# Pairs of split activations moved by 2 to 7 lines of 64 bytes against the weights

## What is computed

```python
# first block: modulation, then three branches of one projection
hx, hc = modulate(rms_norm(x), sh1, sc1), modulate(rms_norm(ctx), csh1, csc1)
... = split_cols(hx @ w_in)             # attention, gated delta rule, gates
x = x + g1 * merge_branches(attn_x, gdn_x, gate_x, w_pa, w_pd, w_out)
x = x + g2 * conv_ffn(modulate(rms_norm(x), sh2, sc2), w_up, ffn_conv_w, ffn_conv_b, w_down)
# second block, two layers
u = rms_norm_2(h, norm1_g[l]); proj = u @ w_in[l]      # pool, differential attention, GLA
h = h + mix @ w_out[l]
z = rms_norm_2(h, norm2_g[l])
h = h + jnp.square(jax.nn.relu(z @ w_mlp1[l])) @ w_mlp2[l]
return rms_norm_2(h, final_norm_g)
```

## Time and profile before

| | |
|---|---|
| median of 3 runs | 2678.33 us (2673.72 to 2687.87) |
| profiled execution | 2682.11 us, its span 2680.3 us |
| mean granted TensorE clock | 0.975 |
| TensorE matmul busy | 2577.4 us, 96% of the span |
| weight loads busy | 2081.2 us, 78% |
| VectorE, ScalarE, GpSimd busy | 1399.7, 1023.4, 277.2 us |
| instructions | 46124, of them 19758 matmuls |

### The profile page before, as it was taken

How to read it: one execution, slowest core, us unless ns; L and a number is a source line. 1 busy time by engine, 2 the same in 40 slices (tenths; PEclk the granted TensorE clock), 3 DMA queues, 4 the chain that set the end, 5 groups by cost and what they waited for, 6 DMA issues and landing times.

```text
span 2680.3 us, 46124 instructions
## 1 busy us (share of the span) xinstructions
PE 2577.4 (96%) x19758; PEld 2081.2 (78%) x19758; DVE 1399.7 (52%) x1950; ACT 1023.4 (38%) x1697; POOL 277.2 (10%) x228
## 2 busy tenths in 40 slices
PE   6998999999998999899999999999999999999998
PEld 5755787778987788688888877788888876788887
DVE  4345698545677433566653546553453446552542
ACT  3245665423334322333333436432233346431222
POOL 0210102223331000111101001100001001100001
PEclk8999999979999999999999989999999999999999
DMA  6100310131003233222323211233232211223322
GB/s 263 57 16 20 114 56 33 65 128 66 4 4 134 86 101 104 101 95 95 98 93 100 87 56 48 79 102 95 95 101 96 87 48 48 95 94 99 98 95 71
DMA packets 64715, 222.91 MB, mean 83 GB/s; under 512 B 7168, under 2 KB 7552, under 8 KB 64384
## 3 DMA queue, kind: packets, MB, share of 16 engines
q1 hardware_dynamic: 63936, 218.39, 24.3%
q10 hardware_dynamic: 576, 1.57, 0.1%
HBM read 213.64 MB, written 6.29 MB: 82 GB/s over the span
## 4 chain that ended last, share of the span: by engine, by line
PE 89%; DVE 6%; issue 2%; ACT 2%; DMA 1%; POOL 0%; SPq 0%; POOLq 0%; DVEq 0%; ACTq 0%
PE ps L321 59%; PE ps L2696 6%; PE ps L1715 5%; PE ps L331 3%; PE ps L837 2%; PE ps L812 1%; PE ps L1721 1%; PE ps L1740 1%; PE ps L1757 1%; DMA ring<-in_w_mod_first 1%; PE ps L2747 1%; DVE w_lo L299 1%; PE ps L828 1%; PE ps L2777 1%; PE ps L1915 1%
## 5 line engine op out<-in xcount | busy, mean ns | idle before, releaser
L299 DVE TENSOR_TENSOR w_lo<-ring,w_hi 128x1024 fp32r<-128x1024 f32 (+1 forms) x339 | 420.7, 1241 | 835.3 <-ACT w_hi L291 835.2
L291 ACT CAST w_hi<-ring 128x1024 fp32r<-128x1024 f32 (+1 forms) x339 | 353.9, 1044 | 922.1 <-PE ps L321 832.2
L321 PE MATMUL ps<-u_hi,w_hi 128*128 128x512 f32 x864 | 338.7, 392 | 9.0 <-DVE u_lo L580 9.0
L321 PE MATMUL ps<-u_hi,w_lo 128*128 128x512 f32 x864 | 336.9, 390 | 0.0
L321 PE MATMUL ps<-u_lo,w_hi 128*128 128x512 f32 x864 | 336.9, 390 | 0.0
L321 PE MATMUL ps<-mid_hi,w_hi 128*128 128x512 f32 x688 | 267.6, 389 | 0.0
L321 PE MATMUL ps<-mid_lo,w_hi 128*128 128x512 f32 x688 | 267.6, 389 | 0.0
L321 PE MATMUL ps<-mid_hi,w_lo 128*128 128x512 f32 x688 | 267.6, 389 | 0.0
L321 PEld LDWEIGHTS ps<-u_hi,w_hi 128*128 128x128 f32 x864 | 162.5, 188 | 46.8 <-issue 8.9
L321 PEld LDWEIGHTS ps<-u_hi,w_lo 128*128 128x128 f32 x864 | 162.6, 188 | 34.0
L321 PEld LDWEIGHTS ps<-u_lo,w_hi 128*128 128x128 f32 x864 | 162.6, 188 | 33.8 <-issue 0.5
(11 more groups left out here) (449 smaller groups left out, 4677.5 us busy)
## 6 DMA issues: line engine op xcount, KB each, us to landing
ring<-in_w_up SPq DMA_DIRECT2D x44, 512.0 KB, 3.4
ring<-in_w_in SPq DMA_DIRECT2D x42, 512.0 KB, 3.5
ring<-in_w_merge SPq DMA_DIRECT2D x32, 512.0 KB, 3.5
ring<-in_w_mlp1a SPq DMA_DIRECT2D x32, 512.0 KB, 3.5
ring<-in_w_mlp2a SPq DMA_DIRECT2D x32, 512.0 KB, 3.5
ring<-in_w_mlp1b SPq DMA_DIRECT2D x32, 512.0 KB, 3.5
ring<-in_w_mlp2b SPq DMA_DIRECT2D x32, 512.0 KB, 3.5
ring<-in_w_gdn_in SPq DMA_DIRECT2D x24, 512.0 KB, 3.5
```

Source lines behind the costliest of these rows:

```text
L291: nc.scalar.copy(w_hi[:, slot, 0:width], ring[:, n % RING, 0:width]).then_inc(*hi_ok.one())
L299: nc.vector.tensor_tensor(w_lo[:, slot, 0:width], ring[:, n % RING, 0:width], as_f32(w_hi[:, slot, 0:width]), ALU.subtract).then_inc(*lo_o ...
L321: mm = nc.tensor.matmul(dst[:, a:b], w[wi][:, k * P:(k + 1) * P], src[xi][:, k0 + k, a:b], start=start and k == wi == xi == 0, stop=stop a ...
```

## The change

Each pair is allocated behind a small unused tile, its lead, so that it begins a number of lines past a multiple of 512 bytes: `attn_back` 2, `h_lat` 3, `gdn_o` 4, `src` 5, `u` 6, `mid` 7, `mid2` 2, and `h` 0. Hi and lo half have the same number, since each half is a multiple of 512 bytes long. Weights, `ring` and all other large tiles are allocated as before.

```diff
+LEAD = {"h": 0, "attn_back": 2, "h_lat": 3, "gdn_o": 4, "src": 5, "u": 6, "mid": 7, "mid2": 2}
...
+        def lead(ctx, name, side="left"):
+
+            lines = LEAD[name]
+            taken[name + "_lead"] = taken.get(name + "_lead", 0) + 1
+            n = taken[name + "_lead"]
+            words = 16 * (lines if side == "left" else (ROW // 64 - 1 - lines) % (ROW // 64))
+            if words:
+                ctx.enter_context(nc.sbuf_tensor(f"{name}_lead{n}", [P, words], F32, side=side,
+                                                 align_bytes=ROW if side == "left" else 64))
+
         def far_pair(ctx, name, *shape):
 
+            lead(ctx, name, "right")
             taken[name] = taken.get(name, 0) + 1
             return tuple(ctx.enter_context(nc.sbuf_tensor(f"{name}_{part}{taken[name]}", [P, *shape], F32R, side="right",
-                                                          align_bytes=ROW))
+                                                          align_bytes=64))
                          for part in ("hi", "lo"))
...
-                xs = src if given else (sbr(s, "src_hi_buf", nk, LAT), sbr(s, "src_lo_buf", nk, LAT))
+                xs = src if given else split_pair(s, "src", nk, LAT)
...
         def split_pair(ctx, name, *shape):
-            return sbr(ctx, name + "_hi", *shape), sbr(ctx, name + "_lo", *shape)
+
+            lead(ctx, name)
+            return tuple(ctx.enter_context(nc.sbuf_tensor(f"{name}_{part}{taken.get(name + '_lead', 0)}", [P, *shape],
+                                                          F32R, align_bytes=64)) for part in ("hi", "lo"))
```

## The result

The kernel with the leads takes 2713.23 us (median of 4 runs, 2705.8 to 2723.32), the kernel before 2677.55 us (median of 4, 2673.72 to 2687.87). The ratio is 1.013, with an interval of 1.0086 to 1.0173: slower by 35.7 us. The forecast was 2679 us and no change, with a range of 2642 to 2716 us. The profiled execution took 2723.32 us, with a span of 2721.4 us and a granted clock of 0.974. Its span is 41.1 us longer than the one before; 7.1 us of that lie ahead of the first product that was moved (it starts at 847.8 us for 840.6, with a granted clock of 0.90 for 0.97 between 600 and 700 us), and 34.0 us behind it.

The account below looks back on a forecast made before the run. TensorE's matmul count times a 226.7 ns spacing was taken as the bound. The profiled 2682.1 us changed by 0, and the forecast was set near the three-run median, at 2679 us, range 2642 to 2716 us.

Parts of the forecast that it names:

- rival C: Moved tiles enter one more 512-byte stretch, each product pays: 2713 us at 5 ns, 2771 us at 13.5 ns; chance 0.17.
- What bounds the kernel: TensorE, busy 96% of 2680.3 us; long runs are a matmul count times 226.7 ns, and only the spacing can change.
- First, which matmuls: 6912 products of 512 columns get another address, plus 384 in line 331 whose weights move; each nanosecond is 6.9 us.
- Second, the spacing: Spacing of the 6912 products and the 384 unchanged, 0, by nearest rows with operands 4 lines and 1 line apart.
- The last part of the prediction: Expected 226.7 ns chain rows after; fails if a moving tile's start matters, which no earlier row tests.
- The upper and lower ends: On the 6912 products, the constant 13.5 ns goes wholly, -93 us, or is paid twice, +93 us.
- The estimate of 215.8 ns: Skill's spacing for back-to-back 512-column products, against 226.7 ns in the trace; 75 us if gained, not used in the sum.
- Third and fourth, the other engines and the neighbours: VectorE and ScalarE accesses to pairs taken at 0, no DMA changes; all other large tiles stay on multiples.
- A: Reads of moving tile and next weights collide at equal starts, leads end it: 9.9 ns a product, 2610 us; chance 0.08.
- B: A holds for some line numbers only: `u` at 6 lines gains 33 us, 2645 us; chance 0.09.
- D: `u`, allocated from the end of memory, lands at another number of lines than 6; changes no time by itself.

Follow-up runs that it names:

- Experiment 1: Against the kernel before: all pairs but `h`, and the split weights and `tabs`, 3 lines past a multiple of 512 bytes; 2676.5 us, ratio 0.9988.
- experiment 3: The changed kernel with only the 6 lines of `u` kept, all other pairs at 0; 2699.56 us, ratio 1.0067 to the kernel before.
- experiment 2: Against the kernel before: only the split weights and `tabs` 3 lines past a multiple of 512 bytes, all pairs on it; 2687.31 us, ratio 1.0038.
- experiment 4: The changed kernel with other leads: 1, 4, 5 and 7 lines spread over the pairs, `h` at 0; one run of 2685.94 us.
- experiment 5: Against the kernel before: only `w_lo` (and `tabs`) 3 lines past the multiple, pairs and `w_hi` on it; one run of 2703.37 us.
- experiment 8: Against the kernel before: only lo halves moved, `mid_lo` by 1 line, first `mid2_lo` by 4, second by 3; one run of 2677.65 us (before: 2682.2).

## Why the prediction went wrong, and what of it was right

The forecast was no change, and the kernel lost 35.7 us. 2713.23 us lies inside the range of 2642 to 2716 us, but only since rival C, with a price of 5 ns, had been taken into it. Experiment 1 refutes the mechanism of C. That the range holds the time is luck.

**What bounds the kernel**: right. In its long runs the time is a count of matmuls times a spacing, and each nanosecond is 6.9 us: 5.1 ns on 6912 products are 35 us, measured 35.7. Not all of them ran at 226.7 ns, though: `u` in line 2696 had 229.5, and the move added only 2.8 to that.

**First, which matmuls**: right, 6912; experiment 3 shows that the price adds by count. The 384 of line 331 are included with a small part: its pieces of 24 products of 512 columns went from 5.47 to 5.59 us, 5 ns each (here the weights are what is moved, by 6 lines). The 144 with 256 columns on `h` kept their time, and after:

```profile
55.77 17.28 PE ps L343 x144
```

Those are not moved. The 192 of `u` with 256 columns, where the distance is 6 lines the other way, pay no price: 118.7 ns in the mean (18 gaps from 1539.79 us on take 2.14 us), 119.9 before.

**Second, the spacing**: this is the step that failed. It took "0 for the 6912 products and for the 384, as these rows are nearest", and the term is 5.1 ns in the mean, from 1.8 (`gdn_o`, 4 lines) to 6.7 (`mid`, 7 lines). The thought that only a distance between two operands could matter was right, and experiments 1 and 2 show it. The rows could not bear the 0, for two reasons that the runs showed:
- The earlier trace rows have a distance of 4 lines. That is the cheapest distance besides 0 (226.7 ns for `mid` in experiment 4, 228.4 for `gdn_o` after). Lines that start to start 0.24 and 0.23 us apart among other work could also not have told 2 ns.
- The earlier trace rows have a distance of 1 line, but in the fp32 kind, which doesn't feel the distance (experiment 2, 592 ns at 3 lines further). They say nothing on the kind that is moved. Their moving tile is also 1 line behind the weights, which in that kind is the place of 3 lines ahead, 6.6 ns.
So no row tested 1, 2, 3, 5, 6 or 7 lines in the kind that matters, and all of the 6912 products but the 192 of `gdn_o` were at such a distance. The last part of the prediction named this hole ("which no row of before tests") and put the wrong operand in it; the chance of 0.17 for a loss was too small for it.

**The upper and lower ends**, 93 us either way from the 13.5 ns that don't grow with the product's length: the loss was at most 6.7 ns at whole lines and 9.9 at 3.75, and no gain was found at any distance for 512 columns. That 13.5 ns are there however long the product is, and 106.6 ns are the work of 256 columns, holds for these rows alone: at 3 lines experiment 2 has 113.5 ns for 256 columns and 233.2 for 512, a difference of 119.7. So within one line of the kernel the distance moved the two lengths in opposite directions, by -6.4 and +5.7 ns, and the part that doesn't grow with the length isn't one number. What the 13.5 ns are stays open. The estimate of 215.8 ns from the Trainium skill ("TensorE: Matmul & The Clock Gate", the section on the measured 56 ns gap) was met by no kind of 512-column product here.

**Third and fourth, the other engines and the neighbours**: right. VectorE's write of `u_lo` is within 1 ns, the wait for it within 0.2 us, and in experiment 3 all other kinds keep their spacing.

**The rivals.** A and B need a distance that is faster than 0: 0.25, 0.5, 0.75, 1 to 7, 3.5 and 3.75 lines were tried, and none is for the 512 columns that 6912 products have. What they describe exists in the small part: 256 columns at 3 lines, 6.4 ns less, which is 1.2 us for the 192 on `u`. C gave 2713 us by a price of 5 ns, and 2713.23 was measured; but its mechanism is refuted by experiment 1, where all the moved tiles enter the extra stretch of 512 bytes and nothing is lost. The price came from line 1868 (394 ns for 389), whose distance of 4 lines is the harmless one and whose 5 ns have no shown cause, so that it fits is chance. D did not occur: `u` pays what 2 lines pay, as 6 should.

The same page of the Trainium skill (the step on LDWEIGHTS) has TensorE read weights and moving operand through two independent ports, so that a load doesn't slow the product. The prediction used it against A. The runs fit it only in part: the load is hidden (187/188/193 ns after), but where the two start within 256 bytes changes the spacing of the products by up to 6.7 ns, or 9.9 at 3.75 lines. A collision of the two reads would explain that it depends on the distance alone and repeats; this is argued, not shown, and it doesn't explain by itself why 256 columns gain where 512 lose.

**Left open**: whether a product meets the load of its own or of the next weights (experiments 5 and 8 fit neither); why products of 256 columns are faster at 3 lines; why distances that change from product to product can cost more than their parts; why the 512 columns of `h` keep 231 ns at a distance of 0 and of 3 lines behind; what makes two patterns at 2 and 6 lines. No version beat the kernel before: distances of 0 and 4 lines are the best found, and the change should be taken back.

## What to carry to other kernels

Keep the moving tile of a 512-column float32r product at the same start modulo 256 bytes as its weights; both 3 lines past a multiple are as good as both on it, and other distances cost 2 to 10 ns on 227, 1 to 4% of those products' time (1.3% of this kernel). Measure other column counts by themselves: 256 columns were fastest at 3 lines. Before a row is taken as evidence that an edit costs nothing, ask whether it has the same kind of instruction and the same number as the edit: here one row had the kind and a harmless number, the other a dear number and an insensitive kind. A uniform train of matmuls is a good gauge, since a piece of the chain divided by its count gives the spacing to 0.1 ns (348.22 us for 1536 before and in experiment 1).

## What was not expected of the hardware

- The spacing of 512-column float32r products depends on the distance of the two operands' starts modulo 256 bytes: 226.7, 228.9, 232.4 to 233.3, 233.3 ns at 0, 1, 2, 3 lines of 64 bytes, and 231.7 to 233.5 at a quarter to three quarters of a line, 235.2 to 236.6 at 3.75 lines.
- It isn't symmetric: 1 line ahead costs 2.2 ns, 1 line behind (3 ahead) 6.6 to 6.7. Line 347 of experiment 4, with the moving weights 1 line behind, has 233.3 ns, line 346 of experiment 2, with them 3 ahead, 233.2.
- The same products with 256 columns go the other way: 119.9 ns at 0, 118.7 at 2 lines, 113.5 at 3 (all on `u`; on `h` 120.0 and 117.8). Only the 256-column products of `h` that alternate with 512-column ones rose, from 116.6 to 119.3, with the weights 3 lines ahead (experiment 1). The fp32 kind (592 ns each) shows nothing.
- The gaps in a slow train are uneven, 227 to 242 ns at 2 lines, while a train at distance 0 has 226 and 227 throughout; and one program can have either of two patterns, 232.4 or 233.3 ns in the mean.
